# Two experts side by side in the halves of TensorE's columns, with plain float32 products

## The chip, the cores and the metric

One Trainium2 chip, one core. The metric is the device time of one execution in microseconds (us); the kernel before was run three times.

## The reference, cut to what matters

Two blocks run one after the other. The first has two layers of attention and a mixture of 16 experts, of which each of the 256 tokens uses two; the second has two more layers with a dense feed-forward stage. The change touches only the experts:

```python
def grouped_moe(h, router_w, router_b, w_gate, w_up, w_down):   # h [1, 256, 1024]
    ...                      # gate [.., 16]: two nonzero weights per token
    for e in range(N_EXPERTS):                                  # 16
        hid = jax.nn.silu(h @ w_gate[e]) * (h @ w_up[e])        # 1024 -> 512
        out = out + gate[..., e:e + 1] * (hid @ w_down[e])      # 512 -> 1024
    return out
```

All data are float32. Each layer has its own weights: 3 matrices of 2 MB for each expert.

## The kernel before, in words

**Slots of tokens.** For every expert, up to `CAP` = 64 tokens are gathered into slots by a product with a 0/1 matrix `pick` (256 tokens by 64 slots). If some expert had more than 64 tokens, `rounds` would repeat the stage; otherwise its `If` is skipped. The experts go in `PAIRS` = 8 pairs, in a loop `Fori(0, PAIRS)` over `i`, and inside it one expert after the other (`d` = 0, 1). TensorE gathers both experts of the next pair together (`gather`, 128 slots wide, eight chunks of 128 features), so `xT` holds 64 columns of expert 0 beside 64 of expert 1.

**Split products.** `copy` on ScalarE (L1315) rounds a unit of 128x1024 weights to the fp32r type (`high_part`, into one of four buffers `w_hi` that live in `hT_r` and `y_r`); `tt` on VectorE (L1701) writes the rest in place into the weights' own slot `ring_r` (`low_part`). An expert has `UNITS_E` = 12 such units. The tokens are split in the same way (`gathered` and `gathered_rest`, `hidT_hi` and `hidT_lo`, `got_hi` and `got_lo`). TensorE then makes three fp32r products where there was one, in `split_products`:

```python
mm(o, x_hi[:, k, :], hi[:, j, :], k == 0, False)
last = mm(o, x_lo[:, k, :], hi[:, j, :], False, False)
...
ins = mm(o, x_hi[:, k, :], lo[:, j, :], False, k == n - 1)
```

The stationary operand is 64 columns wide (the slots of one expert), the moving one 512 wide (the weights), and the result lies in PSUM partitions 0 to 63. Gate and up have 8 chunks each, down has 4 chunks for each of two halves of 512 outputs: 24 x 3 = 72 such products an expert, 144 a pair.

**Around them.** VectorE makes `hid` from `sil`, the slot's gate and the up product (L1707). TensorE transposes it, ScalarE and VectorE split it, and the down product follows. `scatter` adds an expert's result to the 256 tokens in PSUM banks 0 to 3, by fp32r products with `pickT`; it is put off to a place where TensorE would otherwise wait.

**Weights.** The SBUF area `ring` has six slots of 2 MB, three for each expert of a pair, one set only. `expert_loads` on SyncE waits until an expert's gate and up products are done (`gu_mm`), then issues the loads of the same two matrices of the expert two further on; for down it waits for `dn_mm`. The first pair's loads are issued in the order of the slots 0 to 5, as the stages ahead free the slots (`first_free`).

**Elsewhere.** All matmuls are recorded under L704, the helper `mm`. A plain float32 product shows as two records of TensorE, an fp32r product as one. The feed-forward stages of the second block also use split products and aren't touched, but their counts of `hi_ready` and `lo_ready` start at `FF_UNITS`, which the change sets to zero. The out projection (`mix_mm`) and the PLE products (`ple_mm`), ahead of the experts, are plain float32 products with a 128-wide stationary operand. DIFF attention makes its scores from 64 rows of the array, first four products in rows 0 to 63 and then four in rows 64 to 127; SB attention alternates between the two row halves from head to head.

Of the kernel before, what the change touches and what calls it, by code (L numbers as in the profile page):

```python
# [6 lines left out]
F32 = mybir.dt.float32  # L7
# [40 lines left out]
UNITS_E = 12  # L48
# [102 lines left out]
def program(nc, A, out):  # L151
    ctx = ExitStack()
    with ctx:
# [80 lines left out]
        pickT_all = view(2304, 2 * NT * P, of=arena_r)[0:CAP]  # L234
        pickT = [pickT_all[:, d * NT * P:(d + 1) * NT * P].rearrange("p (t s) -> p t s", t=NT) for d in range(2)]

        xT_hi, xT_lo = (view(a, KC * 2 * CAP, of=arena_r) for a in (2816, 3840))
        sil = view(4864, DE)[0:CAP]
        hid = view(5376, DE)[0:CAP]
        hidT_hi, hidT_lo = (view(a, FC * CAP, of=arena_r) for a in (5888, 12864))  # L240
        got_hi, got_lo = (view(a, DM, of=arena_r)[0:CAP] for a in (9728, 11840))
        zero_f = view(9472, 256)
        zeros = zero_f.bitcast(mybir.dt.bfloat16)

        w_hi = [(hT_r, y_r)[i // 2][:, (i % 2) * UNIT:(i % 2 + 1) * UNIT].rearrange("p (k n) -> p k n", k=2) for i in range(HI_BUFS)]

        def unit(of, d, q):

            n = 3 * d + q // 4
            v = of[:, n * SLOT_W:(n + 1) * SLOT_W]  # L250
            if q < 8:
                return v.rearrange("p (k n) -> p k n", k=KC)[:, 2 * (q % 4):2 * (q % 4) + 2, :]
            half, f = 1 - (q - 8) // 2, 2 * (q % 2)
            return v.rearrange("p (k n) -> p k n", k=FC)[:, f:f + 2, half * 512:half * 512 + 512]
# [44 lines left out]
        slot_gate = tiny(2)[0:CAP]  # L299
# [171 lines left out]
        sel_ready, xg_mm, xg_ev, tr_mm, tr_ev = (sem(n) for n in ("sel_ready", "xg_mm", "xg_ev", "tr_mm", "tr_ev"))  # L471
        gu_mm, sil_ev, hid_ev, ht_mm, ht_ev = (sem(n) for n in ("gu_mm", "sil_ev", "hid_ev", "ht_mm", "ht_ev"))
        xg_hi, ht_hi, hi_ready, lo_ready, unit_used = (sem(n) for n in ("xg_hi", "ht_hi", "hi_ready", "lo_ready", "unit_used"))
        gt_mm, gt_ev, got_hi_ev, round_done = (sem(n) for n in ("gt_mm", "gt_ev", "got_hi_ev", "round_done"))
        dn_mm, got_ev, sum_done = sem("dn_mm"), sem("got_ev"), sem("sum_done")
        out_done = sem("out_done")

        MOE_TURNS = NE // 2

# [34 lines left out]

        FF_UNITS = [DEPTH * ROUNDS * NE * UNITS_E + 8 * FF_CHUNKS * L for L in range(DEPTH)]

# [43 lines left out]
        def _(sp):  # L560
            sp.dma_start(consts[:, :], A["consts"][:, 0:CONST1]).then_inc(const_load, 16)

            def wait_last_experts(l, n):
                last = l * ROUNDS * NE + NE - 2 + n // 3
                if n % 3 < 2:
                    sp.wait_ge(gu_mm, last + 1)
                else:
                    sp.wait_ge(dn_mm, 2 * last + 2)

            for l in range(DEPTH):  # L570
# [25 lines left out]
                first_free = [(mix_mm, 4 * l + 2), (mix_mm, 4 * l + 4), (ple_mm, 8 * l + 8), (ple_mm, 8 * l + 8),  # L596
                              (ple_mm, 8 * l + 8), (u_mm, NU * l + U_LAST[5])]
                for d in range(2):
                    for j, (name, k) in enumerate((("w_gate", KC), ("w_up", KC), ("w_down", FC))):
                        n = 3 * d + j  # L600
                        sp.wait_ge(*first_free[n])
                        sp.dma_start(slot(n, k), A[name][l, d].rearrange("(k p) n -> p k n", p=P)).then_inc(slot_full[n], 16)

                def expert_loads(R, r, first):
                    with sp.Fori(first, MOE_TURNS) as i:
                        for d in range(2):
                            for j, (name, k) in enumerate((("w_gate", KC), ("w_up", KC), ("w_down", FC))):
                                n = 3 * d + j

                                if j < 2:  # L610
                                    sp.wait_ge(gu_mm, i * 2 + R * NE + (d - 1))
                                else:
                                    sp.wait_ge(dn_mm, i * 4 + R * (2 * NE) + (2 * d - 2))
                                src = A[name][l].rearrange("e (k p) n -> e p k n", p=P)[bass.ds(i * 2 + d, 1)].rearrange("e p k n -> (e p) k n")
                                sp.dma_start(slot(n, k), src).then_inc(slot_full[n], 16)
# [5 lines left out]
                with sp.If(crowded == 1):  # L621
# [3 lines left out]
                    sp.wait_ge(dn_mm, 2 * NE * ROUNDS * (l + 1))  # L625
# [76 lines left out]
        def _(pe):  # L702
# [15 lines left out]
            for l in range(DEPTH):  # L718
# [170 lines left out]
                def gather(G, c0):  # L889
# [6 lines left out]
                def slot_gates(col):  # L896

                    for e in range(2):
                        for t in range(NT):
                            ins = mm(ps[0:CAP, 7, 2 * e:2 * e + 2], pick[:, t, e * CAP:(e + 1) * CAP], gate_w[:, bass.ds(col + t * JOBS, 2)], t == 0, t == NT - 1)  # L900
                    ins.then_inc(gt_mm, 1)

                def split_products(o, x_hi, x_lo, d, q, k0, n, U):


                    pe.wait_ge(lo_ready, U + (q + 1))
                    hi, lo = w_hi[q % HI_BUFS], unit(ring_r, d, q)
                    for j in range(2):
                        k = k0 + j
                        mm(o, x_hi[:, k, :], hi[:, j, :], k == 0, False)  # L910
                        last = mm(o, x_lo[:, k, :], hi[:, j, :], False, False)
                        if j == 1:
                            last.then_inc(unit_used, 1)
                        ins = mm(o, x_hi[:, k, :], lo[:, j, :], False, k == n - 1)
                    return ins

# [1583 lines left out]
```

## Time and profile before

| | us |
|---|---|
| three runs: median (lowest, highest) | 2412.16 (2410.68, 2413.51) |
| profiled execution: span from first to last instruction | 2401.6 |
| what the median has beyond that span | 10.6 |
| TensorE busy (share of the span) | 2061.2 (86%) |
| VectorE busy | 1346.5 (56%) |
| ScalarE busy | 918.0 (38%) |
| chain that ended last: TensorE's share | 78% |
| mean granted TensorE clock over the span | 0.895 of full |

The span runs from the first instruction of the core to the last; what an execution takes ahead of the first instruction and behind the last is in the runs' times and not in the span, and the profile gives no other time of the profiled execution. Busy times of engines overlap each other. TensorE's records are pipelined: the busy time of a group is less than its count times its mean, and the step from one start to the next is what a product costs in a row of products. The page's 40 slices are about 60 us each; the two expert stages fill slices 5 to 11 and 16 to 22.

### The profile page before, as it was taken

The numbers are of one execution on the slowest core, as the hardware profiler recorded it, in microseconds if no ns is written. First come the engines' busy times: TensorE is split into PE (matmuls) and PEld (weight loads), VectorE is DVE, ScalarE is ACT, GpSimd is POOL, SyncE is SP. The second block draws the span as 40 slices with busy tenths as digits, with TensorE's granted clock in tenths as the row PEclk, the third lists the DMA queues.
The fourth block names the chain that finished last, engine by engine and source line by source line (L and its number), as shares of the span: only waits on it lengthen the run. The fifth ranks groups of instructions, "written<-read, shape, count | busy, mean of one in ns | idle before, by whom it ended". The sixth has DMA issues, their size and how long they took to land.

```text
span 2401.6 us, 27982 instructions
## 1 busy us (share of the span) xinstructions
PE 2061.2 (86%) x10511; PEld 1503.8 (63%) x10515; DVE 1346.5 (56%) x2274; ACT 918.0 (38%) x1304; POOL 0.4 (0%) x6
## 2 busy tenths in 40 slices
PE   7858999999968689999997798768588997786998
PEld 5544566666656545666664546658537996354998
DVE  7752377777631434877876635555515564424565
ACT  1131376777512303767764115112013342132443
POOL 0000000000000000000000000000000000000000
PEclk9867999999989589999998796789788998988999
DMA  7033387777802125777776200000051544201342
GB/s 250 28 131 99 141 292 263 283 264 267 289 19 101 62 88 195 266 281 266 286 282 227 100 2 1 1 1 1 1 210 55 191 153 162 105 1 35 141 179 83
DMA packets 153215, 348.09 MB, mean 145 GB/s; under 512 B 8096, under 2 KB 15136, under 8 KB 153136
## 3 DMA queue, kind: packets, MB, share of 16 engines
q1 hardware_dynamic: 145616, 338.28, 39.0%
q10 hardware_dynamic: 7520, 8.75, 1.2%
q8 instruction: 50, 0.82, 0.1%
q14 instruction: 29, 0.24, 0.0%
HBM read 345.97 MB, written 1.05 MB: 144 GB/s over the span
## 4 chain that ended last, share of the span: by engine, by line
PE 78%; DVE 12%; issue 4%; ACT 4%; DVEq 1%; DMA 0%; another core or an unknown queue 0%; ACTq 0%
PE ps L704 74%; DVE ring L1701 2%; DVE arena L1701 2%; DVE bias L1707 1%; DVE h L1707 1%; PE ps L711 1%; PE ps L1002 1%; DVE arena L1707 1%; ACT arena L1511 1%; PE ps L1045 1%; DVE small L1707 1%; ACT arena L1315 0%; DMA arena<-in_rel_bias 0%; DVE ring L1707 0%; DVE small L1704 0%
## 5 line engine op out<-in xcount | busy, mean ns | idle before, releaser
L704 PE MATMUL ps<-ring,hT 128*128 128x512 f32 (+5 forms) x864 | 357.1, 574 | 11.6 <-DMA ring<-in_mla_w_ukv 8.1
L1701 DVE TENSOR_TENSOR ring_r<-ring,y_r 128x1024 fp32r<-128x1024 f32 x256 | 307.3, 1219 | 46.5 <-ACT y_r L1315 45.5
L704 PE MATMUL ps<-ring_r,arena_r 128*64 128x512 f32 x768 | 302.6, 394 | 0.0
L1315 ACT ACTIVATE y_r<-ring 128x1024 fp32r<-128x1024 f32 x256 | 266.6, 1053 | 88.4 <-PE ps L704 88.4
L704 PE MATMUL ps<-arena_r,ring_r 128*128 128x272 f32 (+1 forms) x1024 | 294.2, 287 | 0.0
L1701 DVE TENSOR_TENSOR ring_r<-ring,hT_r 128x1024 fp32r<-128x1024 f32 x192 | 230.9, 1221 | 102.0 <-ACT hT_r L1315 101.4
L704 PEld LDWEIGHTS ps<-ring,hT 128*128 128x128 f32 (+1 forms) x864 | 159.6, 187 | 202.1 <-issue 186.7
L704 PE MATMUL ps<-hT_r,arena_r 128*64 128x512 f32 x768 | 245.1, 401 | 2.1 <-DVE small L2006 2.1
L1315 ACT ACTIVATE hT_r<-ring 128x1024 fp32r<-128x1024 f32 x192 | 201.9, 1059 | 111.7 <-PE ps L704 89.7
L704 PE MATMUL ps<-y_r,arena_r 128*64 128x512 f32 x768 | 239.0, 393 | 0.0
L704 PEld LDWEIGHTS ps<-arena_r,ring_r 128*128 128x128 f32 x1024 | 196.0, 191 | 0.0
L704 PE MATMUL ps<-arena_r,ff_hi_r 128*128 128x272 f32 (+1 forms) x992 | 186.2, 285 | 2.8 <-DVE arena L1701 2.8
L704 PE MATMUL ps<-arena_r,y_r 128*128 128x272 f32 (+1 forms) x544 | 152.6, 292 | 26.5 <-DVE ring_r L1701 23.4
L1315 ACT ACTIVATE arena<-ps 128x256 f32<-128x256 f32 (+7 forms) x118 | 48.4, 442 | 327.3 <-PE ps L704 293.7
L704 PE MATMUL ps<-ring 128*128 128x128 f32 (+2 forms) x848 | 133.5, 325 | 40.2 <-DVE ring L1701 30.3
L704 PEld LDWEIGHTS ps<-arena_r,ff_hi_r 128*128 128x128 f32 x992 | 154.8, 189 | 3.2 <-DVE arena L1701 3.2
L704 PEld LDWEIGHTS ps<-hT_r,arena_r 128*64 128x64 f32 x768 | 101.9, 136 | 81.4 <-issue 14.9
L704 PEld LDWEIGHTS ps<-ring_r,arena_r 128*64 128x64 f32 x768 | 104.0, 135 | 75.2 <-issue 2.0
L704 PEld LDWEIGHTS ps<-ring 128*128 128x128 f32 (+2 forms) x848 | 118.1, 221 | 52.3 <-DVE ring L1701 30.0
L704 PEld LDWEIGHTS ps<-y_r,arena_r 128*64 128x64 f32 x768 | 102.8, 134 | 73.8
L704 PE MATMUL ps<-hT_r,y_r 128*128 128x272 f32 (+1 forms) x480 | 140.0, 292 | 0.0
L704 PE MATMUL ps<-hT,ring 128*128 128x256 f32 (+1 forms) x576 | 129.4, 387 | 0.4 <-DVE hT L1701 0.4
(269 smaller groups left out, 2579.5 us busy)
## 6 DMA issues: line engine op xcount, KB each, us to landing
ring<-in_w_gate SPq DMA_DIRECT2D x32, 2048.0 KB, 8.4
ring<-in_w_up SPq DMA_DIRECT2D x32, 2048.0 KB, 13.4
ring<-in_w_down SPq DMA_DIRECT2D x32, 2048.0 KB, 7.9
ring<-in_w_ff SPq DMA_DIRECT2D x32, 2048.0 KB, 8.3
ring<-in_w_in SPq DMA_DIRECT2D x8, 2048.0 KB, 16.5
ring<-in_w_in_ab SPq DMA_DIRECT2D x5, 2048.0 KB, 8.8
ring<-in_w_o SPq DMA_DIRECT2D x4, 2048.0 KB, 10.9
ring<-in_ple_gate SPq DMA_DIRECT2D x4, 2048.0 KB, 19.2
```

What stands on the lines that cost most here:

```text
L704: return pe.matmul(o, lhsT, rhs, start=a, stop=z)
L711: ins = pe.transpose(ps[:, g, j * P:(j + 1) * P], src[:, t, (c0 + j) * P:(c0 + j + 1) * P], ident)
L1002: ins = pe.transpose(ps[:, b, o:o + rows(t)], un[0:rows(t), t, c * P:(c + 1) * P], ident[0:rows(t), 0:rows(t)])
L1045: ins = pe.transpose(ps[0:rows(b), 4 + b, hd * P:hd * P + r], probs[i % 2][0:r, hd, cols(b)], ident[0:r, 0:r])
L1315: return act.activation(o, i, ACT.Copy, scale=scale)
L1511: link(act.activation(sq_junk, h[:, t, :], ACT.Square, scale=DM ** -0.5, accum_out=ss2[:, t:t + 1]))
L1701: return dve.tensor_tensor(o, a, b, op)
L1707: return dve.scalar_tensor_tensor(o, a, s, b, op0, op1, accum_out=acc)
```

## The change

The two experts of a pair are worked on together. For each chunk of features there are two plain float32 products: expert 0 writes PSUM partitions 0 to 63 and expert 1 partitions 64 to 127 of the same bank, one after the other in program order. `sil`, `hid`, `hidT`, `got` and `slot_gate` are now 128 partitions (or columns) wide, one set for both experts. `high_part`, `low_part`, `w_hi`, `unit` and all the other splitting are gone; gathers, transposes and scatters also go by pairs, and the scatter is plain float32. The loads of a pair's two gate matrices are issued together once the gate products of the pair ahead are done, then the two of up, then the two of down.

```diff
-                def split_products(o, x_hi, x_lo, d, q, k0, n, U):
-                    pe.wait_ge(lo_ready, U + (q + 1))
...
+                    def both(bank, x, n, j, chunks):
+                        for k in range(chunks):
+                            for d in range(2):
+                                e = slice(d * CAP, (d + 1) * CAP)
+                                ins = mm(ps[e, bank, :], x[:, k, e], n(3 * d + j)[:, k, :], k == 0, k == chunks - 1)
+                        return ins
...
+                    with pe.Fori(0, PAIRS) as i:
+                        pe.wait_ge(xg0_ev, i + R * (PAIRS + 1) + 1)
+                        pe.wait_ge(xg1_ev, i + R * (PAIRS + 1) + 1)
+                        weights_in(i, 0)
+                        both(6, xT, lambda n: slot(n, KC), 0, KC).then_inc(gu_mm, 1)
+                        pe.wait_ge(gt_ev, i + R * (PAIRS + 1) + 1)
+                        weights_in(i, 1)
+                        both(7, xT, lambda n: slot(n, KC), 1, KC).then_inc(gu_mm, 1)
+                        pe.wait_ge(got0_ev, i + R * (PAIRS + 1) + 1)
+                        for t in range(NT):
+                            ins = pe.transpose(ps[:, 4, t * P:(t + 1) * P], pick[:, t, :], ident)
+                        ins.then_inc(tr_mm, 1)
+                        pe.wait_ge(got1_ev, i + R * (PAIRS + 1) + 1)
+                        scatter()
+                        pe.wait_ge(hid_ev, i + R * PAIRS + 1)
+                        for f in range(FC):
+                            ins = pe.transpose(ps[:, 6, f * P:(f + 1) * P], hid[:, f * P:(f + 1) * P], ident)
+                        ins.then_inc(ht_mm, 1)
+                        pe.wait_ge(sel_ready, i + R * (PAIRS + 1) + 2)
+                        slot_gates(i * 2 + 2)
+                        gather(0)
+                        pe.wait_ge(tr_ev, i + R * PAIRS + 1)
+                        gather(4)
+                        pe.wait_ge(ht_ev, i + R * PAIRS + 1)
+                        weights_in(i, 2)
+                        for half in (1, 0):
+                            pe.wait_ge((xg1_ev, xg0_ev)[half], i + R * (PAIRS + 1) + 2)
+                            both(4 + half, hidT, lambda n: slot(n, FC)[:, :, half * 512:half * 512 + 512], 2, FC).then_inc(dn_mm, 1)
```

SyncE, the first pair and the others:

```diff
-                first_free = [(mix_mm, 4 * l + 2), (mix_mm, 4 * l + 4), (ple_mm, 8 * l + 8), (ple_mm, 8 * l + 8),
+                first_free = [(mix_mm, 4 * l + 2), (mix_mm, 4 * l + 4), (ple_mm, 8 * l + 2), (ple_mm, 8 * l + 4),
                               (ple_mm, 8 * l + 8), (u_mm, NU * l + U_LAST[5])]
...
+                for n in (5, 0, 1, 2, 3, 4):
...
+                        for j, (name, k) in enumerate(EXPERT_PARTS):
+                            if j < 2:
+                                sp.wait_ge(gu_mm, i * 2 + R * NE + (j - 1))
+                            else:
+                                sp.wait_ge(dn_mm, i * 2 + R * NE)
+                            for d in range(2):
```

ScalarE now has, for each pair, the SiLU of the gate product, the copies of `hidT` and `pickT`, the copy of one half of the next `xT` and of one half of `got`; VectorE has `hid`, the four comparisons of `select`, the slots' gates and the other halves:

```diff
+                    with act.Fori(0, PAIRS) as i:
+                        act.wait_ge(gu_mm, i * 2 + R * NE + 1)
+                        act.activation(sil, ps[:, 6, :], ACT.Silu).then_inc(sil_ev, 1)
+                        act.wait_ge(ht_mm, i + R * PAIRS + 1)
+                        copy(hidT.rearrange("p f s -> p (f s)"), ps[:, 6, :]).then_inc(ht_ev, 1)
+                        copy(pickT.rearrange("p t s -> p (t s)"), ps[:, 4, 0:NT * P]).then_inc(tr_ev, 1)
+                        gathered(i * 2 + R * (2 * PAIRS + 2) + 3)
+                        act.wait_ge(dn_mm, i * 2 + R * NE + 1)
+                        copy(got[:, 512:1024], ps[:, 5, :]).then_inc(got1_ev, 1)
```

## Rows read from the trace of the kernel before

**Rows 1.** The page, parts 1 and 4: engine totals, and shares of the last-ending chain.
```profile
PE 2061.2 (86%) x10511; PEld 1503.8 (63%) x10515; DVE 1346.5 (56%) x2274; ACT 918.0 (38%) x1304; POOL 0.4 (0%) x6
...
PE 78%; DVE 12%; issue 4%; ACT 4%; DVEq 1%; DMA 0%; another core or an unknown queue 0%; ACTq 0%
```

**Rows 2.** Stretches view; the two expert stages, first gate product to last product.
```profile
core 0: us, PE busy (x) PEld busy (x) DVE busy (x) ACT busy (x) POOL busy (x), PEclk, DMA share, GB/s
287.20:655.20 368.00, 366.78 (x1792) 236.63 (x1792) 274.78 (x307) 254.95 (x289) 0.00 (x0) 0.98 0.77 278
938.90:1303.80 364.90, 363.69 (x1792) 234.36 (x1792) 274.71 (x307) 254.91 (x289) 0.00 (x0) 0.99 0.76 280
```

**Rows 3.** Chain in order of time, layer 1: start us, us, what.
```profile
1044.39 42.96 PE ps L704 x209
...
1226.99 76.82 PE ps L704 x392
```

**Rows 4.** Groups of instructions, six pairs of layer 1, window 952 to 1227.
```profile
L704 PE MATMUL ps<-ring_r,arena_r 128*64 128x512 f32 x288 | 113.3, 394 | 0.0
...
L1701 DVE TENSOR_TENSOR ring_r<-ring,hT_r 128x1024 fp32r<-128x1024 f32 x72 | 86.5, 1221 | 39.4 <-ACT hT_r L1315 39.4
...
L1315 ACT ACTIVATE y_r<-ring 128x1024 fp32r<-128x1024 f32 x73 | 76.3, 1054 | 10.9 <-PE ps L704 10.9
...
L1707 DVE SCALAR_TENSOR_TENSOR arena<-arena,small,ps 64x512 f32<-64x512 f32 x13 | 9.6, 738 | 4.7 <-ACT arena L1465 4.7
...
L1315 ACT ACTIVATE arena_r<-ps 128x512 fp32r<-128x512 f32 x12 | 7.2, 597 | 14.4 <-PE ps L704 14.4
```

**Rows 5.** Timeline, TensorE, plain float32 out projection: start us, us, work.
```profile
838.59 27.73 PE L704 MATMUL ps<-ring,hT 128*128 128x512 f32 x64 [0.69 <-ACT hT L1315]
```

**Rows 6.** Stretches view; the same stretch.
```profile
838.00:866.00 28.00, 27.41 (x64) 12.08 (x64) 3.56 (x6) 0.54 (x1) 0.00 (x0) 1.00 0.30 87
```

**Rows 7.** Timeline, TensorE: DIFF scores, then stick-breaking (SB) scores, in row halves.
```profile
139.85 5.65 PE L704 MATMUL ps<-arena 64*128 64x256 f32 x16 [3.21 <-DVE small L1704]
150.79 3.09 PE L704 MATMUL ps<-arena 64*128 64x256 f32 x16 [5.29 <-DVE small L1704]
```

**Rows 8.** Stretches view; those two groups, for the granted clock.
```profile
139.80:145.60 5.80, 5.65 (x16) 4.18 (x16) 0.06 (x1) 3.19 (x16) 0.00 (x0) 0.50 0.06 23
150.70:154.00 3.30, 3.09 (x16) 2.64 (x16) 0.11 (x2) 3.23 (x13) 0.00 (x0) 0.50 0.00 0
```

**Rows 9.** Timeline, TensorE, after a gate and up: gather, transposes, gates, gather, scatter.
```profile
1245.73 1.95 PE L704 MATMUL ps<-arena,h 128*128 128x128 f32 x16
...
1249.20 2.05 PE L704 MATMUL ps<-arena,h 128*128 128x128 f32 x16
1251.18 2.11 PE L704 MATMUL ps<-arena_r 64*128 64x512 f32 x8
1253.22 0.67 PE L704 MATMUL ps<-hT_r,arena_r 128*64 128x512 f32 x2
```

**Rows 10.** Timeline, TensorE: transposes of y.
```profile
834.44 3.46 PE L711 MATMUL ps<-consts,y 128*128 128x128 f32 x16 [0.47 <-ACT y L1315]
```

**Rows 11.** Stretches view; weight loads with no gap between them.
```profile
305.00:315.00 10.00, 10.00 (x45) 5.86 (x44) 8.03 (x8) 8.11 (x9) 0.00 (x0) 1.00 1.02 373
350.00:360.00 10.00, 10.00 (x45) 5.77 (x44) 8.23 (x11) 8.03 (x10) 0.00 (x0) 1.00 1.03 391
```

**Rows 12.** The page, part 6: DMA issues.
```profile
ring<-in_w_up SPq DMA_DIRECT2D x32, 2048.0 KB, 13.4
```

**Rows 13.** Timeline, SyncE's queue, before the first pair.
```profile
273.05 0.37 SPq L602 DMA_DIRECT2D ring<-in_w_down  x1
...
277.25 4.76 SPq L602 DMA_DIRECT2D ring<-in_w_down  x1
```

**Rows 14.** Timeline, TensorE, end of layer 0's expert stage.
```profile
656.60 2.09 PE L704 MATMUL ps<-arena_r 64*128 64x512 f32 x8 [1.40 <-DVE arena_r L1701]
663.89 1.48 PE L704 MATMUL ps<-arena 128*128 128x512 bf16 x3 [5.20 <-issue]
```

More of the change, by code:

```diff
@@ L233, in program @@
         pick = view(2048, NT * 2 * CAP, pat="p (t n) -> p t n", t=NT)
[L234 to L241, printed above, removed]
+        pickT = view(2304, NT * P, pat="p (t s) -> p t s", t=NT)
+        xT = view(2816, KC * 2 * CAP, pat="p (k s) -> p k s", k=KC)
+        sil = view(4864, DE)
+        hid = view(5376, DE)
+        hidT = view(11840, FC * 2 * CAP, pat="p (f s) -> p f s", f=FC)
+        got = view(9728, DM)
         zero_f = view(9472, 256)
         zeros = zero_f.bitcast(mybir.dt.bfloat16)
[L245 to L254, printed above, removed]
         ple_sig = view(6144, NT * DM, pat="p (t d) -> p t d", d=DM)
@@ L298, in program @@
         picked = tiny(NT * NE)
[L299 removed]
+        slot_gate = tiny(1)
         slot_of, gate_w = tiny(NT * JOBS), tiny(NT * JOBS)
@@ L513, in program @@
         FF_CHUNKS = D_FF // 512
-        FF_UNITS = [DEPTH * ROUNDS * NE * UNITS_E + 8 * FF_CHUNKS * L for L in range(DEPTH)]
+        FF_UNITS = [8 * FF_CHUNKS * L for L in range(DEPTH)]
         def ff_steps(eng, step):
@@ L896, in slot_gates, with scatter @@
                 def slot_gates(col):
-                    for e in range(2):
-                        for t in range(NT):
-                            ins = mm(ps[0:CAP, 7, 2 * e:2 * e + 2], pick[:, t, e * CAP:(e + 1) * CAP], gate_w[:, bass.ds(col + t * JOBS, 2)], t == 0, t == NT - 1)
-                    ins.then_inc(gt_mm, 1)
-                def split_products(o, x_hi, x_lo, d, q, k0, n, U):
-                    pe.wait_ge(lo_ready, U + (q + 1))
[L907 to L915, printed above, removed]
-                def scatter(d, n):
-                    pe.wait_ge(got_ev, n)
-                    for half in (1, 0):
-                        for part in (got_hi, got_lo):
-                            for t in range(NT):
-                                ins = mm(ps[:, 2 * t + half, :], pickT[d][:, t, :], part[:, half * 512:half * 512 + 512], False, False)
+                    for t in range(NT):
+                        ins = mm(ps[:, 7, 0:2], pick[:, t, :], gate_w[:, bass.ds(col + t * JOBS, 2)], t == 0, t == NT - 1)
+                    ins.then_inc(gt_mm, 1)
+                def scatter():
+                    for half in (1, 0):
+                        for t in range(NT):
+                            ins = mm(ps[:, 2 * t + half, :], pickT[:, t, :], got[:, half * 512:half * 512 + 512], False, False)
                     return ins
@@ L981, in expert_round @@
-                    with pe.Fori(0, PAIRS) as i:
-                        for d in range(2):
-                            expert(i, d)
-                    scatter(1, R * (2 * NE + 2) + (2 * NE + 2)).then_inc(round_done, 1)
-                    pe.wait_ge(xg_ev, R * (2 * PAIRS + 2) + (2 * PAIRS + 2))
+                        pe.wait_ge(sel_ready, i + R * (PAIRS + 1) + 2)
+                        slot_gates(i * 2 + 2)
+                        gather(0)
+                        pe.wait_ge(tr_ev, i + R * PAIRS + 1)
@@ L2055, in expert_round @@
-                    for q in range(4):
-                        low_part(0, 0, q)
-                    for c0 in (0, 4):
-                        gathered_rest(R * (2 * PAIRS + 2) + (1 + c0 // 4), c0)
-                    gates_of_slots(R * (PAIRS + 1) + 1)
-                    with dve.Fori(0, PAIRS - 1) as i:
-                        for d in range(2):
-                            expert(i, d, False)
-                    expert(PAIRS - 1, 0, False)
-                    expert(PAIRS - 1, 1, True)
```

197 lines of the change are left out of this document (54 added, 143 removed).

## The prediction

> **What bounds the kernel now.** I read the page first: TensorE is busy for 86% of the span and is 78% of the chain that ended last [rows 1]. The average hides where that is, so I cut out the two expert stages, from the first gate product to the last down product: 368.0 and 364.9 us, of which TensorE is busy for all but 1.3 us each, at a granted clock of 0.98 and 0.99 of full, while the DMA engines are busy for three quarters and move 280 GB/s [rows 2]. So TensorE sets these 732.9 us. The chain view, in order of time, gives the rhythm: a scatter starts at 1044.39 and the one four pairs later at 1226.99, which is 45.65 us a pair [rows 3]. Grouped by instruction, the stage is the 144 split products of a pair with a 64-wide stationary operand; VectorE and ScalarE split weights behind them at 1.22 and 1.05 us a unit, wait, and hold nobody up for long [rows 4].
>
> **What the new products cost one by one.** The out projection is 32 plain float32 products of the same size in moving columns (512), at full clock: 64 records in 27.73 us, so 0.433 us a record and 0.867 us a product [rows 5, 6]. A 64-wide stationary operand does not shorten this, since the moving operand is streamed. A pair now has 16 products for gate, 16 for up, 16 for down. One after the other they are 13.9 us for each group of 16, 41.6 us in all. If the two experts' products run at the same time in the two halves of the columns, a group is 6.9 us and the three are 20.8 us.
>
> **Do they run at the same time?** No row of the kernel before shows products in different column halves: all its 64-wide ones are in the same half. The nearest rows are plain float32 products in different row halves. The SB scores alternate between the row halves as the new products alternate between the column halves. They are 8 records of 256 moving columns and 8 of 128, at a granted clock of 0.50. At half clock 256 columns cost what 512 cost at full, 0.433 us, and 128 half of that, so one after the other they would take 5.2 us and more; they took 3.09 us. The DIFF scores, 16 records of 256 columns, would take 6.9 us, and took 5.65, although the halves come one after the other in program order [rows 7, 8]. So float32 products in different parts of the array do overlap, fully where they alternate (2.6 us and the last one's tail). What differs is that two column halves each need all 128 partitions of a moving operand of their own, twice the data of two row halves. The two ends for a group of 16 are 6.9 and 13.9 us; I take 6.9, by the row that is nearest.
>
> The Trainium skill ("TensorE: Matmul & The Clock Gate", Part 3, the table of measured speedups) gives 2.38 times for three column tiles; by that, as an estimate, two would give some 1.6 to 2, and the sum would be near mine; no row here can show it. The same part says that a weight load overlaps products in flight only where the row groups differ, or, elsewhere on the page, where it goes to the background buffer. The first half of that speaks against this change, since column halves share their row groups. The trace shows 64 loads, busy 12.08 us, under 64 records of the same rows with no room left between them [rows 6], so here loads do hide. That load may still be exposed in column halves is a rival below.
>
> **The rest of TensorE's work for a pair.** The gather is unchanged: 16 records take 1.88 us and the other 16 take 1.98, start to start; the scatter now takes 2.04 as 8 fp32r products [rows 9] and becomes 4 plain ones, 3.5 us (4 x 0.867), for the whole pair. Six transposes at 0.22 (3.46 / 16) are 1.3 us [rows 10]. The slots' gates are 0.3, and I allow 0.2 for waits. Sum: 20.8 + 3.9 + 3.5 + 1.3 + 0.3 + 0.2 = 30.0 us a pair, against 45.65.
>
> **What hides the rest.** The splitting on ScalarE and VectorE goes. VectorE keeps `hid` (0.74 us), four comparisons and copies of about 0.6 us [rows 4], under 5 us a pair; ScalarE about as much, with its table loads. `hid` is ready 1 us after the up products, and TensorE meanwhile has two transposes and a 3.5 us scatter; without that cover the pair would take 1 us more. The copies of `hidT` and `pickT` lie under the first 1.88 us of gather, those of `xT` under the second half of it and the down products. No wait that I find ends later than the work queued ahead of it.
>
> **The weights.** A pair needs 12.58 MB, and there is one set of slots. Where loads follow each other without a gap they run at 373 and 391 GB/s [rows 11], mean 382, so 32.9 us a pair: more than TensorE's 30.0. So the loads become the bound. Each pair of slots is asked for when its products end, 23 us ahead of when that is next needed, while a load of 4 MB takes 11 us alone; SyncE's queue is in the order in which slots come free, and nothing on it waits behind a later event. From issue to landing the second of two loads takes 13.4 us [rows 12], 11 us of transfer and some 2 of latency. Walked forward pair by pair: the first three steps are TensorE's 30.0 us, because their weights were ahead, the fourth is 31.2, then 32.9, and the stage takes 253 us. At 400 GB/s it would be 244, at 361 (280 / 0.77, the stage's own rate per busy share) 265; with no DMA bound at all, 8 x 30.0 = 240.
>
> The first pair does not stall: the old order issued slot 2 at 273.05 and the last at 277.25 [rows 13], and now slots 5, 2 and 3 are asked for earlier, in a stretch with no DMA. Their last load, slot 4, has the time from 273 until the first up products at 294. At the end of the stage, slots 0 and 1 for the next stage are asked for 23 and 16 us ahead; the others wait for the last down product, 19 us of transfers, and the next stage first needs slot 2 over 28 us later. The last scatter takes 3.5 instead of 2.09 us, and 5.2 us of issue follow it [rows 14], in the `Else` of `rounds`; I leave those. The longer scatter is paid back by the copies ahead of the first gate product, where one copy replaces a copy and a subtraction.
>
> **Sum.** Against the profiled span: 368.0 + 364.9 - 2 x 253 = 227 us less, so a span of 2175 (2401.6 - 227). The median of the runs has 10.6 us more than the span: 2412 - 227 = 2185 us.
>
> **Rivals.**
> - *The columns do not overlap* (the other side). A group is 13.9 us, a pair 50.9 (30.0 + 20.8), a stage 407. That is 81 us more than before over both: 2493. For it: no row shows it otherwise, and the doubled moving data. Against it: the SB scores. It decides from a group of 12.2 us, an overlap of less than 1.14 times, where a pair takes the old 45.7. Chance 0.20.
> - *Half an overlap* (shared reading of moving data): a group 10.4, a pair 40.4, a stage 323: 2412 - 87 = 2325. Chance 0.10.
> - *Weight loads exposed*: 48 records in each half, each with 0.13 us of load ahead of it (the stage's mean load, 236.63 us over 1792 [rows 2]), are 6.3 us a pair: 36.3, a stage 290, 2412 - 152 = 2260. It is what the skill's first half-rule would do here. Chance 0.07.
> - *The clock*: TensorE now waits about 3 us a pair for weights, and the row of the scores shows the lower of the two levels, 0.50, after waits of 3 and 5 us [rows 7, 8]. If the clock stayed low for over two thirds of a pair, 30 us of work would be 45.7 again and nothing would be won. As the work lengthens the waits go, so this corrects itself; near 2412, chance 0.02. A few us of it are inside my range.
>
> **Numbers.** The chances: my forecast 0.61, no overlap 0.20, half 0.10, loads 0.07, no change 0.02. A measurement here cannot tell 0.2% (5 us) from no change. Faster 0.78, same 0.02, slower 0.20. The forecast's own range is 2155 (TensorE's floor of 240 us a stage, with a few us to spare) to 2240. The range for 8 in 10 takes in the two middle cases and half an overlap with some more: 2155 to 2390; it leaves out the no-overlap case.
>
> **What the profile after would show.** Right: a stage of 240 to 265 us; a pair in 30 to 33 us; records of the two experts starting in twos, a group of 32 records in 7 us; the DMA share near 1 in the later pairs, and TensorE waiting there for `ring` from the DMA. A group of 14 us with TensorE busy throughout and the DMA share below 0.7 proves the first rival. Groups of 9 to 10 us with gaps as wide as a load prove the third. The clock row inside the stage settles the fourth. The prediction would be most wrong through the one step that no row shows, the overlap of column halves.

## The result, and the profile after

The changed kernel takes 2161.06 us (median of 4 runs, 2157.56 to 2167.55); the kernel before, on the same chip, 2411.42 (4 runs, 2404.57 to 2413.51). The ratio is 0.897, 95% interval 0.896 to 0.899: 250 us less, and 24 less than the forecast of 2185. The profiled execution took 2157.56 us with a span of 2155.8, so 1.8 us lie outside the span. Every later profile has the same 1.8 (2462.3 and 2464.08, for one). The 10.6 us by which the median of the kernel before exceeds its profiled span were therefore mostly spread between runs, and not time outside the span.

The page, parts 1 and 4, to be read against [rows 1]:

```profile
PE 1800.6 (84%) x9255; PEld 1241.6 (58%) x9259; DVE 833.1 (39%) x1792; ACT 460.8 (21%) x812; POOL 0.4 (0%) x6
...
PE 66%; DVE 13%; DMA 10%; issue 4%; ACT 4%; SPq 2%; another core or an unknown queue 1%; DVEq 1%; ACTq 0%
```

TensorE's busy time falls by 261 us. DMA, which was 0% of the chain, is now 10%.

The stretches view, the two expert stages (against [rows 2]), then 160 us from the middle of the first stage:

```profile
core 0: us, PE busy (x) PEld busy (x) DVE busy (x) ACT busy (x) POOL busy (x), PEclk, DMA share, GB/s
286.20:533.40 247.20, 236.93 (x1168) 107.06 (x1168) 24.19 (x72) 30.29 (x47) 0.00 (x0) 0.99 0.99 373
810.00:1058.80 248.80, 236.91 (x1168) 107.02 (x1168) 24.11 (x72) 30.29 (x47) 0.00 (x0) 0.99 0.99 371
...
340.00:500.00 160.00, 152.62 (x748) 68.85 (x746) 15.48 (x45) 21.61 (x32) 0.00 (x0) 0.98 1.04 394
```

The stages lose 120.8 and 116.1 us, 236.9 of the 245.8 us by which the span is shorter. In them the DMA share goes from 0.77 to 0.99, and to 1.04 in the middle, at 394 GB/s; TensorE has 10 to 12 us of idle time in each.

The timeline of TensorE in the first stage (start, length, what, count of records; in brackets the idle time ahead of it and what ended it):

```profile
286.23 13.95 PE L690 MATMUL ps<-ring,arena 128*64 128x512 f32 x64 [0.73 <-DVE arena L1934]
300.12 0.44 PE L924 MATMUL ps<-consts,arena 128*128 128x128 f32 x2
300.39 3.60 PE L690 MATMUL ps<-arena 128*128 128x512 f32 x8
303.83 0.60 PE L932 MATMUL ps<-consts,arena 128*128 128x128 f32 x4
304.26 0.51 PE L690 MATMUL ps<-small,arena 128*128 x4
304.63 3.82 PE L690 MATMUL ps<-arena,h 128*128 128x128 f32 x32
308.38 20.82 PE L690 MATMUL ps<-ring,arena 128*64 128x512 f32 x96
...
366.52 13.95 PE L690 MATMUL ps<-ring,arena 128*64 128x512 f32 x64
383.17 8.78 PE L690 MATMUL ps<-ring,arena 128*64 128x512 f32 x32 [2.69 <-DMA ring<-in_w_up]
...
400.14 13.95 PE L690 MATMUL ps<-ring,arena 128*64 128x512 f32 x64
415.10 7.09 PE L690 MATMUL ps<-ring,arena 128*64 128x512 f32 x32 [1.00 <-DMA ring<-in_w_up]
...
510.87 7.09 PE L690 MATMUL ps<-ring,arena 128*64 128x512 f32 x32 [2.69 <-DMA ring<-in_w_up]
```

The first row is gate and up of the first pair: 64 records in 13.95 us, 7.0 us for each group of 32. Then come two transposes, the scatter, four transposes, the slots' gates and the gather. The row of 96 is down, and gate and up of the next pair. Where 64 records end in a gap, they are down and the next gate, and the 32 behind the gap are up. The wait is for the weights of up.

The clock in and behind one such wait, by the stretches view:

```profile
380.00:385.00 5.00, 2.31 (x10) 0.83 (x8) 0.00 (x0) 0.60 (x1) 0.00 (x0) 0.85 1.04 405
385.00:390.00 5.00, 5.00 (x20) 1.81 (x18) 0.00 (x0) 0.00 (x0) 0.00 (x0) 0.81 1.03 410
390.00:400.00 10.00, 10.00 (x60) 6.67 (x56) 1.71 (x7) 1.47 (x3) 0.00 (x0) 1.00 1.04 390
```

After this wait of 2.7 us the granted clock is below full for a few us, and the 32 records take 8.78 us instead of 7.09. Not every such wait does this: of the seven of 2.7 us in the two stages four are followed by 8.78 us and three, as at 510.87, by 7.09. After a group of 8.78 us the next pair waits only 1.0 us; after one of 7.09 us it waits 2.7 again. The starts of the up groups are 31.93 us apart either way (383.17 to 415.10), which is 12.58 MB at 394 GB/s: the loads set the step, and what the clock takes the wait gives back. Only behind a stage's last wait is it lost. The first stage, whose last up group takes 7.09 us, is 1.6 us shorter than the second, whose last takes 8.78.

The loads view of the timeline, weight loads under the first gate products:

```profile
286.71 0.15 PEld L690 LDWEIGHTS ps<-ring,arena 128*64 128x64 f32 x2 [0.28 <-issue]
287.14 0.15 PEld L690 LDWEIGHTS ps<-ring,arena 128*64 128x64 f32 x2 [0.28 <-issue]
```

### The profile page after: what moved, and what is told of

Same layout as the page of the kernel before. It is cut to its first block, busy times and chain, and to the rows that moved or that the text cites. A ratio compares the mean times of both kernels' runs of the same rounds, so it can differ in the third digit from the quotient of the medians.

```text
span 2155.8 us, 23213 instructions
## 1 busy us (share of the span) xinstructions
PE 1800.6 (84%) x9255; PEld 1241.6 (58%) x9259; DVE 833.1 (39%) x1792; ACT 460.8 (21%) x812; POOL 0.4 (0%) x6
## 4 chain that ended last, share of the span: by engine, by line
PE 66%; DVE 13%; DMA 10%; issue 4%; ACT 4%; SPq 2%; another core or an unknown queue 1%; DVEq 1%; ACTq 0%
PE ps L690 62%; DMA ring<-in_w_up 9%; DVE ring L1634 2%; SPq L601 2%; DVE arena L1634 2%; DVE bias L1640 1%; DVE h L1640 1%; PE ps L964 1%; PE ps L697 1%; ACT arena L1444 1%; PE ps L1007 1%; DVE small L1640 1%; DMA arena<-in_rel_bias 1%; ACT hT L1277 1%
## 5 line engine op out<-in xcount | busy, mean ns | idle before, releaser
L690 PE MATMUL ps<-ring,arena 128*64 128x512 f32 (+3 forms) x1656 | 382.3, 595 | 25.3 <-DMA ring<-in_w_up 21.8
L690 PEld LDWEIGHTS ps<-ring,arena 128*64 128x64 f32 (+1 forms) x1656 | 136.3, 145 | 255.4 <-issue 250.8
L1277 ACT ACTIVATE arena<-ps 128x256 f32<-128x256 f32 (+6 forms) x184 | 82.9, 478 | 634.5 <-PE ps L690 400.5
L690 PE MATMUL ps<-arena 128*128 128x512 f32 (+9 forms) x460 | 134.4, 474 | 42.7 <-DVE small L1637 21.5
L690 PEld LDWEIGHTS ps<-arena 128*128 128x128 f32 (+4 forms) x464 | 81.2, 233 | 82.6 <-issue 38.1
L690 PEld LDWEIGHTS ps<-hT,ring 128*128 128x128 f32 x576 | 110.5, 192 | 19.6 <-issue 1.0
L690 PEld LDWEIGHTS ps<-arena_r,y_r 128*128 128x128 f32 x544 | 104.2, 195 | 27.4 <-issue 27.4
L690 PEld LDWEIGHTS ps<-hT_r,y_r 128*128 128x128 f32 x480 | 94.0, 196 | 0.0
L1634 DVE TENSOR_TENSOR arena<-arena,ps 128x512 f32<-128x512 f32 (+3 forms) x50 | 54.0, 1091 | 103.4 <-PE ps L690 66.8
L1634 DVE TENSOR_TENSOR ring_r<-ring,y_r 128x1024 fp32r<-128x1024 f32 x64 | 76.7, 1222 | 33.3 <-ACT y_r L1277 32.6
## 6 DMA issues: line engine op xcount, KB each, us to landing
ring<-in_w_o SPq DMA_DIRECT2D x4, 2048.0 KB, 11.6
```

Source lines behind the costliest of these rows:

```text
L690: return pe.matmul(o, lhsT, rhs, start=a, stop=z)
L1277: return act.activation(o, i, ACT.Copy, scale=scale)
L1634: return dve.tensor_tensor(o, a, b, op)
```

## Experiments

Times are device us, the median where there are several runs. A stage is measured from the start of the first gate product to the end of the last down product. The runs of the kernel before on the same chips gave 2409, 2411 and 2405.

| kernel | runs | us | ratio to before, 95% | stages, us |
|---|---|---|---|---|
| both experts in one half | 1 | 2464.08 | | 397.1, 397.1 |
| one expert, then the other | 1 | 2281.61 | | 305.8, 305.7 |
| blocks of four, no loads | 1 | 2179.27 | | 252.6, 252.6 |
| half of each up matrix | 2 | 2134.63 | 0.886 (0.884 to 0.889) | 232.3, 232.3 |
| no loads after the first pair | 2 | 2133.94 | 0.886 (0.884 to 0.889) | 232.3, 232.3 |
| changed kernel again | 5 | 2166.57 | 0.900 (0.898 to 0.901) | 246.8, 248.8 |
| changed kernel, third time | 5 | 2164.40 | 0.899 (0.897 to 0.901) | 248.9, 248.8 |
| old order of the first loads | 5 | 2173.19 | 0.901 (0.898 to 0.903) | 248.5, 249.1 |
| seventh slot | 5 | 2166.05 | 0.899 (0.897 to 0.900) | 246.7, 244.6 |
| seventh slot, gate in halves | 5 | 2162.09 | 0.897 (0.895 to 0.898) | 244.5, 244.2 |
| seventh slot, asked for last | 5 | 2174.07 | 0.903 (0.901 to 0.905) | 247.7, 248.8 |
| the same, gate in halves | 5 | 2173.77 | 0.904 (0.902 to 0.906) | 247.6, 248.8 |

### Both experts in one half of the columns

```diff
-ins = mm(ps[e, bank, :], x[:, k, e], n(3 * d + j)[:, k, :], k == 0, k == chunks - 1)
+ins = mm(ps[0:CAP, bank, :], x[:, k, e], n(3 * d + j)[:, k, :], k == 0 and d == 0, k == chunks - 1 and d == 1)
```

> The changed kernel, but the products of both experts write PSUM partitions 0 to 63, so both use the same half of the columns; count, order and size of products, loads and waits stay. (The second expert's result is added to the first's in place of going to partitions 64 to 127, so the output is not that of the reference.) Theory, the gain is the overlap of the two column halves: a group of 16 products goes from 6.98 to 13.9 us, a pair from 29.0 us of TensorE's work to 50, a stage from 248 to about 400, the time from 2161 to about 2465 us, slower than the kernel before. Rival, the gain came from dropping the split products and their helpers, and a 64-wide plain product is cheap by itself: the time stays near 2161 us.

Measured: 2464.08 us. TensorE's timeline, the first gate and up, and the 96 records of down, gate and up in the next pair:

```profile
287.19 27.68 PE L690 MATMUL ps<-ring,arena 128*64 128x512 f32 x64 [0.73 <-DVE arena L1934]
...
323.06 41.41 PE L690 MATMUL ps<-ring,arena 128*64 128x512 f32 x96
```

The same products, weights and loads in one half take 27.68 us where two halves take 13.95, a factor of 1.98. The gain rests on the overlap: without it, the splitting dropped and all else the same, the kernel is 55 us slower than before. That is the first rival of the prediction, made real (it gave 2493).

### How far back the overlap reaches

One expert's products of a group, then the other's:

```diff
-for k in range(chunks):
-    for d in range(2):
+for d in range(2):
+    for k in range(chunks):
```

> The changed kernel with the two loops of a group exchanged: all chunks of expert 0, then all chunks of expert 1, in gate, up and each half of down. Theory, the overlap reaches only some records back, as the DIFF scores of the kernel before showed (5.65 us where 6.9 would be no overlap and 3.5 a full one): about 3 of 16 records overlap where the halves change, a group of 16 products takes about 11 us, a pair 41, a stage 325, the time about 2315 us. Rival one, each half has a queue of its own and the order in the program does not matter: 2161 us. Rival two, only neighbours in program order overlap: a group 13.4 us, a stage 390, the time about 2450 us.

Measured: 2281.61 us, neither of the ends, and 33 less than the 2315 that were expected:

```profile
285.59 22.70 PE L690 MATMUL ps<-ring,arena 128*64 128x512 f32 x64 [0.73 <-DVE arena L1934]
...
316.48 29.79 PE L690 MATMUL ps<-ring,arena 128*64 128x512 f32 x96
```

The 96 records have 7 changes of half (one in each of down's two halves of outputs, in gate and in up, and one where each group follows another). They save 41.41 - 29.79 = 11.62 us, 27 records at 0.4325, so 3.8 records at each change. TensorE's weight loads fit this reach. The loads view of the timeline has one every 0.43 us, and from 290.79 more than one at a time, though the first half's 16 records, one after the other from 285.59, would end only at 292.5, four records later:

```profile
290.36 0.14 PEld L690 LDWEIGHTS ps<-ring,arena 128*64 128x64 f32 x1 [0.29 <-issue]
290.79 0.19 PEld L690 LDWEIGHTS ps<-ring,arena 128*64 128x64 f32 x3 [0.29 <-issue]
291.22 0.19 PEld L690 LDWEIGHTS ps<-ring,arena 128*64 128x64 f32 x2 [0.23 <-issue]
```

A second kernel put a number on this: blocks of four products (eight records) of one expert, then four of the other, with no loads behind the first pair.

```diff
+order = [(k, d) for b0 in range(0, chunks, 4) for d in range(2) for k in range(b0, b0 + 4)]
+for k, d in order:
```

> How far back does the overlap of the column halves reach? As the changed kernel with no loads after the first pair (all pairs use the first pair's weights, so the output is not the reference's), and the products in blocks of four of one expert, then four of the other, where the changed kernel alternates one by one. The first study of this, all of one expert's products of a group and then the other's, gave 3.8 records of overlap at each change of half (27 over the 7 changes among 96 records). If the reach is that, whatever the block's length, the 11 changes here save 42 of 96 records: 41.4 - 11 x 3.8 x 0.4325 = 23.3 us for the 96, a pair of 31.5, a stage of 260 and 2172 in all against 2134 for the kernel without loads. The rival: a block of 8 records is too short to matter and all 96 take 20.8 us as when they alternate, 2134; or the overlap exists only between neighbours (2 records a change) and the 96 take 32 us.

```profile
285.69 16.06 PE L689 MATMUL ps<-ring,arena 128*64 128x512 f32 x64 [0.73 <-DVE arena L1934]
...
309.94 23.15 PE L689 MATMUL ps<-ring,arena 128*64 128x512 f32 x96
333.30 3.60 PE L689 MATMUL ps<-arena 128*128 128x512 f32 x8
...
341.29 23.15 PE L689 MATMUL ps<-ring,arena 128*64 128x512 f32 x96
```

Measured: 23.15 us for the 96 (23.3 expected), a pair of 31.35, 2179.27 in all (2172 expected). (41.41 - 23.15) / 0.4325 / 11 = 3.8 records again. So the saving is the same at each change of half for blocks of 8 and of 16 records. What limits it to 3.8 isn't shown. The stage of 260 us in that expectation was a slip: 8 pairs of 31.5 are 252, and 252.6 was measured.

### What the loads cost

```diff
 # from the second pair on, only the first half of each up matrix
+if j == 1:
+    sp.dma_start(slot(n, k)[:, 0:k // 2, :], src[:, 0:k // 2, :]).then_inc(slot_full[n], 16)
```

> The changed kernel, but from the second pair on only the first half of each up matrix is loaded (1 MB of 2; the rest stays that of the first pair, so the output is not that of the reference). A pair then loads 10.5 MB in place of 12.6. Theory, the later pairs of a stage are bound by bytes at 394 GB/s: 10.5 MB need 26.6 us, less than TensorE's 29.0, so a pair takes 29.0 us instead of 32.0, a stage 233 instead of 248, the time about 2131 us, with TensorE's waits for the DMA gone. Rival, TensorE waits because of the order in which slots are asked for and the latency, not the bytes: steps stay near 32 us and the time near 2161 us.

```diff
 # no loads from the second pair on
-sp.dma_start(slot(n, k), src).then_inc(slot_full[n], 16)
+sp.sem_inc(slot_full[n], 16)
```

> The changed kernel, but no weights are loaded from the second pair on; SyncE counts up the semaphores in place of the loads (all pairs use the first pair's weights, so the output is not that of the reference). Theory, below the loads lies TensorE's own time and nothing else: 29.0 us a pair as in the first pairs, a stage 232, the time about 2129 us, the same as with half of the up weights left out. Rival, the loads' traffic into SBUF also slows the two streams that the halves read: a group of 16 products falls below 6.98 us and the time clearly below 2125 us.

Measured: 2134.63 and 2133.94 us. The waits view for TensorE over the first stage, for the changed kernel and then for half of each up matrix (us in total, times, longest):

```profile
PE ps L690 <- DMA ring<-in_w_up: 10.1, 5, 2.7
PE ps L690 <- DVE arena L1934: 0.7, 1, 0.7
```

```profile
PE ps L693 <- DVE arena L1937: 0.7, 1, 0.7
```

The 96 records of down, gate and up with no loads, to be read against the row at 308.38 above:

```profile
308.84 20.82 PE L689 MATMUL ps<-ring,arena 128*64 128x512 f32 x96
```

Two different cuts, one in which the DMA engines still carry 359 GB/s between 340 and 500 us and one in which they carry 3, end at the same stage of 232.3 us with 29.0 us a pair. So the traffic as such doesn't slow the products; only the waits do. They cost 248 - 232.3 = 15 to 16 us a stage: 10 to 12 us of waiting, and most of the rest the lower clock behind two of the longer waits.

### The order of the first loads

```diff
-first_free = [..., (ple_mm, 8 * l + 2), (ple_mm, 8 * l + 4),
+first_free = [..., (ple_mm, 8 * l + 8), (ple_mm, 8 * l + 8),
...
-for n in (5, 0, 1, 2, 3, 4):
+for n in range(NSLOT):
```

> The changed kernel as it is, as the base for the three beside it on the same chip. Every theory: 2157 to 2168 us, as in its first four runs.

> The changed kernel with the first pair's loads as in the kernel before: slots in the order 0 to 5, slots 2 and 3 asked for only after all PLE products. Four loads of 2 MB then start at about 273 us, 21 us of transfer, so that the last lands at about 296: the first pair's up waits for little or nothing (slot 4 lands at about 291, needed at 293), but the second pair's loads queue some 2 to 3 us behind. Theory, the stage is a queue of bytes from its first load on: every us by which that queue starts later is added, 2 to 3 us a stage, about 5 us in all, near 2166. Rival, the queue has slack in the first three pairs, which TensorE bounds, and swallows it: no change.

Measured: 2166.57 for the changed kernel, 2173.19 with the old order; the intervals overlap, so the time alone doesn't tell them apart. The traces do. With the old order the first gate product of each stage waits 3.3 us for its weights, where it waited 0.73 for VectorE, and gate and up behind that wait take 15.65 us instead of 13.95:

```profile
289.86 15.65 PE L690 MATMUL ps<-ring,arena 128*64 128x512 f32 x64 [3.29 <-DMA ring<-in_w_gate]
...
822.23 15.65 PE L690 MATMUL ps<-ring,arena 128*64 128x512 f32 x64 [3.28 <-DMA ring<-in_w_gate]
```

Both stages (248.5 and 249.1 us) end with an up group of 7.09 us, and are 1.5 to 2.3 us longer than those of the changed kernel that end so (247.0 and 246.8). That is some 4 us a stage in all, where 2 to 3 were expected. Whether loads that queue later or the lower clock of the first group carries through the stage isn't told apart.

The stretch between the stages is 283.9 us with the old order, 283.7 in the kernel before and 276.8, 276.9 and 276.8 in three profiles of the changed kernel. Beside the longer wait, two groups ahead of the second stage differ. The first has 24 records, here with the old order and then in the changed kernel as run again:

```profile
711.51 5.38 PE L690 MATMUL ps<-arena 128*128 128x64 f32 x24 [3.43 <-ACT arena L1381]
```

```profile
708.22 3.81 PE L690 MATMUL ps<-arena 128*128 128x64 f32 x24 [3.43 <-ACT arena L1381]
```

The second has 32. The stretches view of it, in the same order:

```profile
763.70:770.70 7.00, 7.00 (x33) 7.00 (x34) 0.00 (x0) 1.24 (x1) 0.00 (x0) 0.50 0.04 15
```

```profile
758.70:763.50 4.80, 4.79 (x33) 4.79 (x34) 0.00 (x0) 1.26 (x1) 0.00 (x0) 0.76 0.05 20
```

Same work, 2.2 us less, at a granted clock of 0.76 instead of 0.50, after a stretch in which the engine was busy for the same 13.15 us of 23.7. Why the clock is granted there in one kernel and not in the other isn't settled. So of the 7.0 us between the two kernels, 2.6 are the longer wait, which the order of the loads explains, and 3.8 are the clock in these two groups, which no run ties to that order.

### A seventh slot for weights

The SBUF that the split weights left (`hT` and `y`) holds a seventh slot: the gate weights of expert 0 go to slot 0 and to it by turns, in a loop unrolled by two. The load is issued a pair ahead, beside that of expert 1's gate, in front of the up loads.

```diff
+gate_load(slot(3, KC), expert_src("w_gate", i * 4 + (2 * b + 1)), gate3_full, part)
+if ahead:
+    gate_load((spare, slot(0, KC))[b], expert_src("w_gate", i * 4 + (2 * b + 2)), gate_full[1 - b], part)
+rest_of_pair(...)        # up, then down
```

> A seventh slot: hT and y are idle during the stage and together hold 2 MB. The gate weights of expert 0 go by turns into slot 0 and into this spare one, so one load of 2 MB per stage is made ahead of it, and the loop over pairs is unrolled by two. Theory, the stage is bound by bytes from the first gate products on: 86.0 MB in place of 88.1 at 394 GB/s, 5.3 us less a stage, about 10 us in all, near 2151. Rival one, the tail of the stage (last loads, last down products, the If) sets it and not the bytes: no gain. Rival two, the code is twice as long and the Else longer, and instruction loading or semaphores cost what is gained.

> The same with gate weights loaded in halves of 1 MB, the first half asked for once half of the gate products are done. Theory: the queue of bytes starts 3.5 us earlier in each stage, 7 us less than with the spare slot alone, near 2144. Rival, the extra loads and waits of SyncE's queue cost it, or TensorE becomes the bound of the first pairs anyway: as with the spare slot alone.

Measured: 2166.05 and 2162.09, beside 2166.57 for the changed kernel: no gain outside the intervals. TensorE still waits 9.9 us for `ring<-in_w_up` in the first stage, and the up groups still start 31.9 us apart: the load made ahead is in front of up in the queue, so up lands no earlier. Yet the stages aren't the same. Both together they are 491.3 and 488.7 us, against 495.7 to 497.7 in three profiles of the changed kernel. In the last pair no such load stands in front of up, and up doesn't wait there, where it waits 1.0 to 2.7 us in the changed kernel. The time outside the stages is longer by about as much: 1675.1 and 1673.4 us, against 1660.1 to 1669.1. So the theory was in part right about the stages, and what it gained there was lost elsewhere. The wait for up remained, and the obvious cure is the order of need:

```diff
-if ahead:
-    gate_load(...)
 rest_of_pair(...)
+if ahead:
+    gate_load(...)
```

> The kernel with the seventh slot once more, with one load moved: the gate weights for expert 0 of the next pair are asked for behind the down weights of this pair, no longer in front of its up weights. The queue is then in the order in which TensorE needs the matrices. If that order is what kept the slot from paying, the up weights land 5.3 us earlier than with the slot before (2.1 MB at 394 GB/s), TensorE no longer waits for them in most pairs, and a stage takes some 241.5 us instead of 246.8: 10 us less over both, near 2156 beside the changed kernel's 2166 on the same chip, 0.895 of the kernel before. The rival: the stage is bound by the sum of the bytes, whatever their order; then it stays at 246 to 247 us and the time within 2 us of the changed kernel's.

> The same, and the gate weights come in halves of 1 MB, expert 1's first half asked for when half of the gate products are done (3.5 us earlier). If TensorE still waits at the end of the stage for weights that are asked for late, this takes 2 to 3 us more off a stage: some 240 us, its floor by the pairs of 29.0 us with the first and the last, near 2152. The rival, that the bytes bound it: 246 us a stage and the changed kernel's time.

> The changed kernel as it is, once more, to stand beside the other three on the same chip: 2160 to 2167, a stage of 246 to 248 us.

Measured: 2174.07 and 2173.77 against 2164.40: 9.7 us slower, where 10 us faster was expected. The theory falls. The rival was near with the stage (246 to 247 named, 247.7 and 248.8 measured), but had neither its reason nor the loss. Two things happened. First, the stage didn't shrink. SyncE's timeline, first with the load in front of up, then with it behind down:

```profile
292.18 1.01 SPq L595 DMA_DIRECT2D ring<-in_w_gate  x2
299.03 4.49 SPq L617 DMA_DIRECT2D ring<-in_w_up  x2
314.17 0.92 SPq L617 DMA_DIRECT2D ring<-in_w_down  x2
```

```profile
292.94 0.39 SPq L595 DMA_DIRECT2D ring<-in_w_gate  x1
299.79 1.05 SPq L617 DMA_DIRECT2D ring<-in_w_up  x2
314.94 0.92 SPq L617 DMA_DIRECT2D ring<-in_w_down  x2
316.06 6.26 SPq L595 DMA_DIRECT2D ring<-in_w_gate  x2
```

The stretches view over those 24 us, in the same order:

```profile
293.00:317.00 24.00, 24.00 (x126) 11.36 (x124) 3.10 (x9) 3.35 (x5) 0.00 (x0) 1.00 1.01 362
```

```profile
293.00:317.00 24.00, 24.00 (x126) 11.47 (x124) 3.09 (x9) 3.74 (x6) 0.00 (x0) 1.00 0.78 268
```

Slot 0 is free when the first gate products end, ahead of the issues at 292.18 and 292.94, but behind down its load is issued only at 316.06, because SyncE stands before the wait for the first down products (314.94). The DMA engines carry 268 instead of 362 GB/s there, 94 x 24 us = 2.3 MB: about the one matrix (2.1 MB) by which the seventh slot was ahead. In front of up the lead is kept and spent on a matrix that nothing waits for; behind down it is not kept. An issue between up and down might keep both; that wasn't tried.

Second, time is lost outside the stages. TensorE's timeline behind the second stage, the changed kernel (third profile), then the seventh slot asked for last:

```profile
1070.59 1.87 PE L690 MATMUL ps<-arena 128*128 128x512 bf16 x4 [3.79 <-issue]
...
1229.21 4.16 PE L690 MATMUL ps<-arena,ring 128*128 128x64 f32 x24
```

```profile
1075.56 1.86 PE L756 MATMUL ps<-arena 128*128 128x512 bf16 x4 [9.38 <-issue]
...
1234.17 6.55 PE L756 MATMUL ps<-arena,ring 128*128 128x64 f32 x24
```

The first pair of rows is 5.6 us more of idle time that no engine or DMA ended ("issue"), seen behind the second stage and not the first. All four kernels with the slot show it (9.4 to 10.1 us, against 3.8 to 4.2 without the slot). The rival that longer code costs what is gained isn't ruled out by this; what the idle time is made of, the trace doesn't show. The second pair is a group in the second block's attention that takes 6.55 us instead of 4.16, twice (the granted clock of 35 us around them is 0.55; of the like 30 us in the changed kernel, 0.67). This isn't tied to the slot: with the slot and the gate in halves it comes once in one profile, and the kernel with the old order of loads, without the slot, has it twice. The kernels with no loads and with half of each up matrix have it once. A third loss is of the same kind, a group between the stages that takes 11.97 us instead of 9.73, in three of the four kernels with the slot. From the last down product to the end the four kernels with the slot take 1110 to 1111 us in three profiles and 1105 in one, and the changed kernel 1097 to 1104 in three. So of the 9.7 us, 5.6 are idle time that every kernel with the slot shows, and the rest is clock, part of which comes and goes without the slot too.

## Why the prediction was right, point by point

- **What bounds the kernel.** TensorE in the two stages: 236.9 of 245.8 us came from there.
- **A record of 0.433 us and full overlap.** Right: 6.9 us forecast for a group, 7.0 measured; 20.8 for the three, and the 96 records take 20.82 us where TensorE doesn't wait. In one half they take 41.41 (forecast 41.6). That column halves overlap as row halves do was the one step that no row showed; the prediction took it by likeness to the scores and gave it a chance of 0.61. Those rows [rows 7, 8] pointed the right way, and more closely than the prediction used them: DIFF's blocks of eight overlapped in part and SB's alternating ones fully. DIFF saved 1.3 us at its one change of half, some three of its records of 0.433 us, which is near the 3.8 found here.
- **The rest of a pair.** 30.0 forecast, 29.0 measured (337.39 - 308.38). The scatter is 3.44 to the next start, against 3.5. The six transposes take 0.27 + 0.43 us and not 1.3: the 16 of [rows 10] ran at a granted clock of 0.55, by the stretches view of 834.40 to 837.90, and the new ones at full. The 0.2 of waits isn't there, and gather and slots' gates are 4.1 instead of 4.2.
- **The loads become the bound.** Right, with the rate a little low: 32.9 us a pair forecast at 382 GB/s, 32.0 measured at 394. A stage was 253 forecast, 247.2 and 248.8 measured, 10 us less over both. The 361 GB/s of the forecast's slowest case is 278 / 0.77, by the first stage's row, and not 280 / 0.77, which is 364. The engine, the tile and the later pairs were as forecast; the matrix waited for is up.
- **The clock.** A few us, as allowed: 1.7 us behind four of the seven waits of 2.7 us in the profiled execution. The low clock corrects itself as the prediction said: the wait that follows is 1.7 us shorter.
- **The first pair.** It doesn't stall, but the prediction counted its new order at nothing against before. The old order under the new products costs a wait of 3.3 us instead of 0.7 at the start of each stage, and some 2 us within it.
- **Outside the stages.** Nothing was forecast; 8.9 us came: 7.1 between the stages, 1.0 ahead of the first and 0.8 behind the second. Of the 7.1, 3.8 are the clock in the two groups shown above, which take 5.38 and 7.01 us in the kernel before as well, and some 2.5 the shorter way to the first gate product from the point where SyncE issues the first loads that wait for the last PLE product (14.2 us before, 11.6 after); the rest is spread thin. Only the part between the stages comes back in all three profiles of the changed kernel. All that lies outside the stages is 1669 us in the one profile before, and 1660, 1669 and 1665 after, so 8.9 us is the most favourable of the three.
- **The sum.** Of the 24 us between forecast and median, 10 are the rate of the loads and the pair, 9 lie outside the stages, and 5 are the 10.6 us beyond the span, of which the runs of after have 5.3. All three terms were too high, so none made up for another; the last two are no larger than the spread of 10 us between the four runs.
- **The rivals.** No overlap, half of it: refuted by the 13.95 us. Weight loads exposed: the loads view has them in twos every 0.43 us, each time 0.15 us busy, and the products show no gap. This is against the half-rule of the Trainium skill ("TensorE: Matmul & The Clock Gate", Part 3) that a load overlaps products only where the row groups differ; here the row groups are the same and the loads were hidden. The 2.38 times that the Trainium skill gives in the same part for three column tiles made, as an estimate, 1.6 to 2 for two; measured is 1.98.

## What to carry to other kernels

Where products have a stationary operand of 64 columns, put two independent ones in the two halves and alternate them one by one: in blocks, each change of half saved only 3.8 records here. When such a change halves the work of an engine, walk the loads forward at once: here they took back 15 us of a stage's gain. Before adding a spare buffer, ask which matrix is waited for and where in the queue the new load will stand: in front of that matrix it shortened no wait but the last pair's, and behind a wait for a later event it lost its lead. And compare several profiles of the same kernel before a few us outside the changed stage are put down to the change: here they differed by 9 us.

## What the runs showed of the hardware

- Float32 products in the two column halves, each with 128 partitions of its own moving data, run fully at the same time: 64 records in 13.95 us against 27.68, though both halves read twice the data at once.
- If they don't alternate, each change of half saves 3.8 records, with blocks of 8 and of 16 records alike (27 over 7 changes, 42 over 11).
- One queue of 2 MB loads carries 394 GB/s for 160 us at a share of 1.04, and this doesn't lengthen a float32 product of 512 columns: 96 records take 20.82 us with the loads (at 308.38, with 396 GB/s beside them) and without.
- In the profiled execution of the changed kernel four waits of 2.7 us were followed by a lower granted clock and 1.7 us more for the next 32 records, and three by neither; no wait of 1.0 us was. Where the loads set the step, only the last such loss of a stage lengthens it.
